# A hybrid decoder block on one Trainium2 core: last sums given to TensorE, adaLN column sums reordered, second expert matrices stored by row pairs

## The reference, cut to what matters

```python
mod = jax.nn.silu(c) @ w_ada[layer] + b_ada[layer]
sh_a, sc_a, gt_a, sh_f, sc_f, gt_f = jnp.split(mod, N_MOD, axis=-1)
h = modulate(rms_norm(x, g_attn[layer]), sh_a, sc_a)
proj = h @ w_in[layer]
...                                   # differential and stick-breaking attention
x = x + gt_a[:, None, :] * y
h = modulate(rms_norm(x, g_ffn[layer]), sh_f, sc_f)
y = hier_moe(h, w_group, b_group, w_erouter, b_expert, w1, w3, w2)
x = x + gt_f[:, None, :] * y
# in hier_moe, for each expert e, weighted by its share of the token:
#   (silu(h @ w1[e]) * (h @ w3[e])) @ w2[e]
```

## Time and profile before

| | |
|---|---|
| median of 3 runs | 648.7 us (648.4 to 653.58) |
| the profiled execution | 650.03 us, of which its span in the trace is 647.7 us |
| PE busy | 544.8 us (84%), 2948 matrix products |
| DVE busy | 294.2 us (45%) |
| ACT, POOL busy | 184.2 us (28%), 88.3 us (14%) |
| moved by DMA | 169.28 MB |
| mean granted TensorE clock | 0.953 of full |

### The profile page before, as it was taken

The page is one execution under the profiler, slowest core; times in us unless marked ns, Lnnn a source line. Parts: engine busy times, 40 slices in busy tenths (PEclk is TensorE's granted clock), DMA queues, the critical chain, the costliest instruction groups (busy, mean ns, idle before and its releaser), DMA issues.

```text
span 647.7 us, 7637 instructions
## 1 busy us (share of the span) xinstructions
PE 544.8 (84%) x2948; PEld 349.2 (54%) x2948; DVE 294.2 (45%) x504; ACT 184.2 (28%) x327; POOL 88.3 (14%) x100
## 2 busy tenths in 40 slices
PE   2499989999998999999999707889999899788765
PEld 1387768677675666664446505444555445344332
DVE  4888670564879538552022283222332223132116
ACT  5256441342453347883042210000000000000011
POOL 8141010000000000000031111111121111110014
PEclk9999989997999999999999856999999999799997
DMA  8986862765242038000931473999999999999974
GB/s 338 395 273 220 317 236 89 264 255 195 66 195 98 2 121 333 1 1 6 418 140 53 174 315 112 404 420 415 416 417 415 415 417 416 418 415 416 388 277 185
DMA packets 46450, 169.28 MB, mean 261 GB/s; under 512 B 7832, under 2 KB 9880, under 8 KB 38228
## 3 DMA queue, kind: packets, MB, share of 16 engines
q1 hardware_dynamic: 36180, 140.81, 54.7%
q0 software_dynamic: 9104, 25.95, 11.3%
q10 hardware_dynamic: 1136, 2.11, 0.8%
HBM read 160.74 MB, written 16.25 MB: 273 GB/s over the span
## 4 chain that ended last, share of the span: by engine, by line
PE 64%; DVE 14%; DMA 9%; SPq 5%; ACT 4%; issue 3%; DVEq 0%; POOLq 0%; ACTq 0%
PE banks L1703 13%; PE banks L1596 9%; PE banks L1717 7%; DMA obuf<-in_w_dram 4%; PE banks L1548 3%; DVE mixT L873 3%; PE banks L1433 3%; PE banks L1434 3%; PE banks L1435 3%; DMA stage<-in_w_ada_dram 3%; PE banks L1532 2%; PE banks L1692 2%; PE banks L1425 2%; PE banks L1426 2%; PE banks L1427 2%
## 5 line engine op out<-in xcount | busy, mean ns | idle before, releaser
L1717 PE MATMUL banks<-stage,work 128*64 128x512 f32 x168 | 61.2, 635 | 9.0 <-ACT work L840 6.3
L838 ACT ACTIVATE work<-banks 128x256 f32<-128x256 f32 x16 | 6.1, 384 | 201.7 <-PE banks L1703 201.7
L1703 PE MATMUL banks<-qkT,work 128*64 128x256 f32 x272 | 62.6, 388 | 0.4 <-DMA stage<-in_w_dram 0.4
L1596 PE MATMUL banks<-stage,mixT 128*128 128x512 f32 x128 | 56.2, 595 | 0.0
L1264 DVE TENSOR_TENSOR work<-banks,gates 128x1024 f32<-128x1024 f32 x15 | 18.4, 1225 | 77.0 <-PE banks L1717 77.0
L1703 PE MATMUL banks<-hT,work 128*64 128x256 f32 x192 | 44.3, 389 | 2.5 <-DMA qkT<-in_w_dram 2.5
L1259 DVE TENSOR_TENSOR work<-work,banks 128x256 f32<-128x256 f32 x16 | 6.7, 421 | 86.6 <-ACT work L838 86.6
L873 DVE SCALAR_TENSOR_TENSOR mixT<-stage,small,mixT 128x1024 f32<-128x1024 f32 x35 | 44.9, 1282 | 1.2 <-DMA stage<-in_w_ada_dram 0.4
L1435 PE MATMUL banks<-hT_hi,w_lo 128*128 128x512 f32 x112 | 44.3, 396 | 0.0
L1433 PE MATMUL banks<-hT_hi,w_hi 128*128 128x512 f32 x96 | 40.4, 421 | 0.0
L585 POOL DMA_INDIRECT pair_rows<-work,tables x15 | 15.1, 1008 | 184.5 <-DVE work L1264 184.5
(11 more groups left out here) (285 smaller groups left out, 1169.0 us busy)
## 6 DMA issues: line engine op xcount, KB each, us to landing
stage<-in_w_dram SPq DMA_DIRECT2D x31, 1024.0 KB, 20.8
qkT<-in_w_dram SPq DMA_DIRECT2D x23, 1024.0 KB, 19.2
stage<-in_w_ada_dram POOLq DMA_DIRECT2D x16, 1024.0 KB, 5.7
hT<-in_w_dram SPq DMA_DIRECT2D x12, 1024.0 KB, 17.9
stage<-in_w_in_dram SPq DMA_DIRECT2D x5, 2048.0 KB, 10.9
val<-in_w_dram SPq DMA_DIRECT2D x10, 1024.0 KB, 18.6
mixT<-in_w_dram SPq DMA_DIRECT2D x10, 1024.0 KB, 18.6
alibi<-in_w_dram SPq DMA_DIRECT2D x5, 1024.0 KB, 22.3
```

Source lines behind the costliest of these rows:

```text
L1596: ins = mm(banks[:, w % 5, :], mixT[:, k, t * P:(t + 1) * P], wv[:, k % 4, half * 512:(half + 1) * 512], start=(k == 0), stop=(k == KD - 1))
L1703: ins = mm(banks[half * C:(half + 1) * C, 2, up * F:(up + 1) * F], heT[:, r, k * P + half * C:k * P + (half + 1) * C], ws[2 * place + half ...
L1717: ins = mm(banks[half * C:(half + 1) * C, 4 + 2 * r + col, :], geT[:, fc * P + half * C:fc * P + (half + 1) * C], w2s[2 * place + half][:, ...
```

## The change

It has four parts.

1. **The end.** DVE evicts pair 15's y (L1331 before) directly after `gated`. The input rows `xr` are added by PE: `add_x(n)` is a product identity x `xr` half into the bank of collected half n, and the collect product accumulates on it. For tile 0 PE adds the first choice too, with `first_w`, a diagonal matrix of its weights that DVE makes once before the pairs. The two first `add_x` stand ahead of pair 15's `w1` products, two between those and its `w3` products, one after the turn of the gated product, three between the halves of the collect products. ACT weights the second choice of tiles 1 and 2 whole and of tile 3 in halves; DVE adds the first choice to it there (`both_choices`), and last the bank (`last_sum`); for tile 0 one operation does both. POOL has no work at the end. The order of the last sums is `LAST_HALVES`; tile 3's rows are loaded as two DMAs of half the columns.
2. **adaLN sums.** The last of the eight additions of the four vectors that need column sums writes its result in column order (`last_by_col`, into `by_col`, the unused half of `mixT`), reading both inputs at a step of 8 floats; PE then takes its chunks of 128 columns without a step.
3. **w2 by row pairs.** `w2` is laid out `(p f) n -> p (f n)`: partition p holds rows 2p and 2p + 1, 8 KB in one piece. To match, `gated` writes its product with even columns first: it reads both inputs at a step of 2 floats.
4. `expert_h` is split into `expert_up`, called twice; for pairs 0 to 14 nothing moves.

```diff
-COLLECT_BANK = (0, 1, 4, 5, 2, 3, 6, 7)
+COLLECT_BANK = (0, 1, 4, 5, 3, 6, 7, 2)
+LAST_HALVES = ((0, 0), (1, 0), (2, 0), (0, 1), (1, 1), (2, 1), (3, 0), (3, 1))
...
-        w2_v = w2.rearrange("l g e (f p) n -> (l g e) p f n", p=P)
+        w2_v = w2.rearrange("l g e (p f) n -> (l g e) p (f n)", f=FC)
...
             for t in range(NT):
-                dst = fin_pair(t)
-                sp.dma_start(dst, y_dram.rearrange("(k t p) n -> t p k n", k=2, p=P)[t]).then_inc(pairs_in[t], 16)
-            for n in range(2 * NT):
+                dst, src = fin_pair(t), y_dram.rearrange("(k t p) n -> t p k n", k=2, p=P)[t]
+                if t < NT - 1:
+                    sp.dma_start(dst, src).then_inc(pairs_in[t], 16)
+                else:
+                    sp.dma_start(dst[:, :, 0:512], src[:, :, 0:512]).then_inc(pairs_in[t], 16)
+                    sp.dma_start(dst[:, :, 512:1024], src[:, :, 512:1024]).then_inc(pairs_tail, 16)
+            for n, (t, half) in enumerate(LAST_HALVES):
...
-            for t in range(NT):
-                pool.wait_ge(fin_a, t + 1)
-                pool.wait_ge(fin_b, t + 1)
-                g.tensor_tensor(xr[:, t, :], xr[:, t, :], fin_pair(t)[:, 1, :], ALU.add).then_inc(fin_p, 1)
...
+            def last_by_col(dst, sums, src):
+                def turned(ap):
+                    return ap.rearrange("p (j k) -> p k j", k=KD)
+                return v.scalar_tensor_tensor(out=dst.rearrange("p (k j) -> p k j", k=KD), in0=turned(src), scalar=cs[:, KD - 1:KD],
+                                              in1=turned(sums), op0=ALU.mult, op1=ALU.add)
...
-                             acc[:, v, :].rearrange("p (j k) -> p k j", k=KD)[:, k, :], ones[:, 0:1],
+                             by_col[:, v, k * P:(k + 1) * P], ones[:, 0:1],
...
-                v.tensor_tensor(ge_act, gact, banks[:, 2, F:2 * F], ALU.mult).then_inc(ge_ready, 1)
+                v.tensor_tensor(ge_act.rearrange("s (f p) -> s f p", f=FC), gact.rearrange("s (p f) -> s f p", f=FC),
+                                banks[:, 2, F:2 * F].rearrange("s (p f) -> s f p", f=FC), ALU.mult).then_inc(ge_ready, 1)
...
+            def add_x(n):
+                t, half = n % NT, n // NT
+                mm(banks[:, COLLECT_BANK[n], :], ident, xr[:, t, half * 512:half * 512 + 512], start=True, stop=False,
+                   skip_group_check=True)
+
             pe.wait_ge(heT_ready, NQ)
-            expert_h(nq + NQ, place, value, 1)
+            add_x(0)
+            add_x(1)
+            expert_up(w1_in, w1s, 0, place, value, 1).then_inc(h1_done, 1)
+            pe.wait_ge(ysb_ready, nq + (NQ - 1))
+            add_x(2)
+            add_x(3)
+            expert_up(w3_in, w3s, 1, place, value, 1).then_inc(h_done, 1)
             expert_geT(nq + NQ)
+            add_x(2 * NT - 1)
```

More of the change, by code:

```diff
@@ L199, in hymba_block @@
         place_w = rt[:, 1424:1432]
+        first_w = rt[:, 1280:1280 + P]
         nought = val[:, 0, 512:1024]
@@ L849, in _ @@
             gate_pair(nq + NQ)
-            for t in range(NT):
+            for t in range(1, NT - 1):
                 act.wait_ge(pairs_in[t], 16)
@@ L853, in _ @@
                              scale=wpair[:, 1, t:t + 1]).then_inc(fin_a, 1)
+            t = NT - 1
+            for half, arrived in enumerate((pairs_in[t], pairs_tail)):
+                act.wait_ge(arrived, 16)
+                second = fin_pair(t)[:, 1, half * 512:half * 512 + 512]
+                a.activation(second, second, ACT.Copy, scale=wpair[:, 1, t:t + 1]).then_inc(fin_a, 1)
         @block.vector
@@ L1331, in _, with both_choices, last_sum @@
                 v.tensor_tensor(ysb[:, 1, part], banks[:, 6 + half, :], gates[:, 1, part], ALU.mult).then_inc(ysb_last, 1)
[L1332 to L1338 removed]
+            def both_choices(t, part, scaled, summed):
+                dve.wait_ge(fin_a, scaled)
+                pr = fin_pair(t)
+                v.scalar_tensor_tensor(out=pr[:, 1, part], in0=pr[:, 0, part], scalar=wpair[:, 0, t:t + 1],
+                                       in1=pr[:, 1, part], op0=ALU.mult, op1=ALU.add).then_inc(fin_b, 1)
+                dve.wait_ge(fin_b, summed)
+            def last_sum(t, half):
+                n, part = half * NT + t, slice(half * 512, half * 512 + 512)
+                dve.wait_ge(collected, n + 1)
+                if t == 0:
+                    dve.wait_ge(pairs_in[0], 16)
+                    v.scalar_tensor_tensor(out=xr[:, t, part], in0=fin_pair(t)[:, 1, part], scalar=wpair[:, 1, t:t + 1],
+                                           in1=banks[:, COLLECT_BANK[n], :], op0=ALU.mult, op1=ALU.add).then_inc(fin_c, 1)
+                else:
+                    v.tensor_tensor(xr[:, t, part], fin_pair(t)[:, 1, part], banks[:, COLLECT_BANK[n], :],
+                                    ALU.add).then_inc(fin_c, 1)
+            for t, half in LAST_HALVES:
+                if t in (1, 2) and half == 0:
+                    both_choices(t, slice(0, D), t, t)
+                elif t == NT - 1:
+                    both_choices(t, slice(half * 512, half * 512 + 512), NT - 1 + half, NT - 1 + half)
+                last_sum(t, half)
         @block.tensor
@@ L1784, in _ @@
                 y_half(col, place, 1).then_inc(y_last, 1)
-            pe.wait_ge(silu_ready, nq + NQ)
-            for n in range(2 * NT):
-                half, t = n // NT, n % NT
-                if t == 0:
-                    pe.wait_ge(ysb_last, half + 1)
-                mm(banks[:, COLLECT_BANK[n], :], collect[:, t, :], ysb[:, 1, half * 512:half * 512 + 512],
-                   start=True, stop=True).then_inc(collected, 1)
+            pe.wait_ge(pairs_in[0], 16)
+            for half in range(2):
+                part = slice(half * 512, half * 512 + 512)
+                if half == 1:
+                    add_x(NT)
+                mm(banks[:, COLLECT_BANK[half * NT], :], first_w, fin_pair(0)[:, 0, part], start=False, stop=False,
+                   skip_group_check=True)
+                pe.wait_ge(ysb_last, half + 1)
+                if half == 1:
+                    add_x(NT + 1)
+                    add_x(NT + 2)
+                for t in range(NT):
+                    mm(banks[:, COLLECT_BANK[half * NT + t], :], collect[:, t, :], ysb[:, 1, part],
+                       start=False, stop=True, skip_group_check=True).then_inc(collected, 1)
 _INS = ["x", "c", "w_ada", "b_ada", "g_attn", "w_in", "q_norm_g", "k_norm_g", "lambda_q1", "lambda_k1",
```

60 lines of the change are left out of this document (29 added, 31 removed).

## The result

| | before | after |
|---|---|---|
| median, measured beside each other on one chip | 650.2 us (20 runs) | 646.7 us (20 runs) |
| lowest and highest | 647.7 to 653.7 us | 643.3 to 649.4 us |
| ratio after / before | | 0.9945, 95% interval 0.993 to 0.9959 |
| the profiled execution | 650.03 us, span 647.7 | 645.13 us, span 643.0 |
| mean granted TensorE clock | 0.953 | 0.960 |

The change makes the kernel 3.6 us faster (interval 2.7 to 4.5), about 0.55%: a gain that is real, and inside the 1% that the prediction called no change. The forecast was 5.9 us. The time lies inside the stated range (639.8 to 647.2), near its upper end. The two profiled executions lie 4.7 us apart in span.

What follows compares the result with a forecast made beforehand. The prediction took the PE-DVE-ACT ring to bound attention, PE then the weight stream the experts, and late eviction and POOL waits the end. Start and attention -3.2 plus end -2.7 gave -5.9, from 648.7 to 642.8 us; range 639.8 to 647.2.

Steps and rivals of the forecast that it cites:

- The start: Mixer's column sums: PE's shorter sums outweigh DVE's stepped additions, -0.3 us.
- The cap of 34.97 us: At the start, the earliest DVE could take the sums' result, since w_lo ends then and waits for ACT.
- if the attention gives under 2 us: A stated sign that the prediction is wrong; start and attention together were forecast at -3.2 us.
- one of the stepped reads dear: Rival: DVE's stepped reads in the column-order additions or in gated cost more than forecast, 644.6 to 647.3 us; chance 0.25.
- The clock after step 3: Half-speed stretch from 150.3 to 156.9 us shrinks with shorter sums: -1.3 us, the middle of 0 to -2.7.
- Steps 3, 6 and 8: Attention steps: column sums -2.0 us at 3 and -0.7 at 8, DVE's stepped operation +1.1 at 6.
- w2 in 8 KB rows: Expert weight stream rises from 416 to 419 GB/s, -1.4 us at the landing of pair 15's w3.
- The slack behind this reading: In pairs 12 to 15 PE waits for the weight stream, leaving it some 6.1 us of slack.
- The rival by which reads at a step of 8 bytes from PSUM are dear: gated costs +0.28 us a pair; 643.4 us, or 647 without slack; within the dear-reads case of chance 0.25.
- The end: After pair 15's products: y evicted early, PE without waits at full clock, POOL's additions gone; -2.7 us in all.
- `add_x` +1.1: Four add_x ahead of pair 15's last products take nearly all the stream gives; PE becomes the bound by 1 us.
- The slower rival: At the end PE waits for tile 0's rows, the clock falls and thirteen products run at half speed: 654 us; chance 0.07.

Runs made afterwards that it cites:

- e5_warm: The changed kernel with nine products whose result nobody reads put between the mixer's two column sums, in PE's wait: 643.11 us, ratio 0.9902 against before.
- e8_again: The changed kernel run once more with no edit: 645.11 us (11 runs), ratio 0.9928 against before.
- e11_warm_step: Changed kernel with nine unused products between the mixer's sums, add_x(3) moved into the wait for gated, three unused products in step 4's wait: 646.68 us, ratio 0.9916.

## Why the prediction was right and wrong

**The start, the step that failed.** The prediction took 1.7 us for the sums from the router's row at 355 us and carried it to 32 us, and counted the mixer's two stepped additions as 0 because "PE's shorter sums give the time back". The sums took 3.57 us there: at the start PE is still at 1.2 GHz, and an unstepped load at that level (333 ns) is as slow as a stepped one (336). The 16 instructions of 1.7 us are a duration at the full level. So only 0.39 us came back. Of the two additions, each 2.06 instead of 1.28, one cost 0.78 and the other some 0.4, the rest of it hidden in a wait for weights that was there before. With 0.2 of late arrival this gives the +1.02 in which -0.3 stood. The cap of 34.97 us, on which the -0.3 rested, was right: with PE awake (e5_warm) DVE takes the result at 35.16, which is 34.96 without the late arrival. The row of the granted clock was the trap: the windows of the start show 1.00, and I read that as PE's speed. The timeline of before had the answer, products of `h @ w_in` at 0.63 us before 41 us and 0.40 after it:

```profile
40.13 0.63 PE L1446 MATMUL banks<-hT_hi,w_hi 128*128 128x512 f32 x1
...
40.99 0.40 PE L1446 MATMUL banks<-hT_hi,w_hi 128*128 128x512 f32 x1
```

Without the arrival this term is off by 1.1 us at 36 us and by 1.3 from 50 us on, of the 2.3 us by which the forecast missed the measured 3.6. The prediction had named its own sign for this: wrong "if the attention gives under 2 us". In the profiled pair start and attention gave 1.5.

**The range and the rival.** That 646.7 lies in the range of 639.8 to 647.2 says little for the mechanism. It falls where the prediction had put "one of the stepped reads dear" (644.6 to 647.3), and that is not what happened: the additions cost +1.03 at step 6, as forecast, and `gated` nothing. Only that rival's clause on the mixer's sums, another 1 us, came true, and for a reason that it did not name: PE gave nothing back.

**The clock after step 3.** The -1.3 was the middle of a range for one fall. The pair has -1.0, and three other terms of the same kind (+0.7, +1.0, -1.5) that the forecast did not have. In this pair they cancel to +0.2; e8_again shows that such terms differ between executions of one program. A mean over the places where falls may land would have been the fair entry, and the second profile of a kernel the way to know that they move. They may be the rest of the miss, some 1.0 us; with medians of one program 1.6 us apart (646.7, 645.1) it cannot be told closer, and it stays open.

**Steps 3, 6 and 8** were right to 0.1 us: -1.9, +1.0 and -0.8. The doubled read was put at +1.1, by choice between bounds of 0 and +2 that came from DVE's and ACT's rows; it measured 1.03 at step 6 (2.31 less 1.28) and 0.78 at the start. The Trainium skill (SBUF — State Buffer, "Door 1: The DMA port swizzle") says that each access crossing to a new line of 16 bytes pays a penalty; the trace agrees, by 2.31 beside 1.28 us.

**w2 in 8 KB rows.** 419 GB/s, worked out as 419; -1.6 us for -1.4. The slack behind this reading was larger than the 6.1 us counted: already between 558.26 and 576.89 a pair took 18.63 us, with PE idle for 2.71 of them and y at the lower level.

**gated.** The rival by which reads at a step of 8 bytes from PSUM are dear is excluded: 421 ns in all sixteen, as before. The rule of the Trainium skill (PSUM — Partial Sum Buffer, "Specifications (TRN2)") is about matmuls; by these 421 ns it does not carry over to this DVE operation.

**The end** was right part by part: `add_x` +1.1, no wait for weights, y evicted at once, no idle PE, full clock, and 2.54 us less from `gated` to the last sum. The slower rival (PE waits for tile 0's rows) did not come up.

**The reference.** The forecast was counted from a median of 3 runs, 648.7. The 20 runs made beside the changed kernel, these three among them, have 650.2. The ratio is the sound figure.

## What to carry over

Before a duration is carried from one stage to another, compare what one instruction of the same form takes in both: at the start of an execution the granted clock of a window does not say that the engine has woken up. Where two engines share a stage, an edit that moves cost from one to the other must be priced at the level that the receiving and the relieved engine have there, stage by stage; here one edit gained 1.9 us at 147 us and lost 0.8 to 1.0 at 32. And work placed in a wait that is there anyway can be free: one product that was going to delay something (0.86 us), or products nobody reads that raise the clock (1.34 us at the start) or keep it up, if they last until the wait ends. It is no sure gain in the time: e11_warm_step kept the clock up in one place and came out no faster.

## What the runs showed of the hardware

- PE ran at 1.2 GHz over the first 38 to 41 us (products of 512 columns at 0.63 us, then 0.40) although the windows there show a granted clock of 1.00. With nine products of 256 columns in its idle time it reached the full level at 29.5 us (634 ns an instruction, then 379).
- A weight load of 128x128 floats at a step of 8 takes 335 ns at full level and 336 at the lower one; without a step 192 and 333. The stepped load took the same time at both levels and the unstepped one did not, so column order helped at the full level alone.
- DVE's `scalar_tensor_tensor` on 1024 elements takes 2.06 to 2.31 us with two inputs and the output as in `last_by_col` (a step of 8 floats), and 1.28 unstepped. With a step of 2 floats, an input in PSUM among them, 256 elements take 0.42 us as before.
- One program had its granted clock fall at different places in two executions, worth 1.0 and 1.3 us, with everything between in step to 0.1 us.
